# Two-layer hybrid token-mixing backbone: a weight split moved behind two stage borders, sixteen transposes moved ahead of another

## The reference

```python
for layer in range(DEPTH):
    p_lat = _split(_modulate(h_x, mod_lat[0], mod_lat[1]) @ w_in[layer], GROUP_COLS)
    p_ctx = _split(_modulate(h_c, mod_ctx[0], mod_ctx[1]) @ w_in[layer], GROUP_COLS)
    y_a = _rwkv7_mixer(p_ctx[0], p_lat[0], ...)
    y_b = _diff_attention(p_ctx[1], p_lat[1], ...)
    y_c = _hgrn2_mixer(p_ctx[2], p_lat[2], ...)
    y_d = _mlstm_mixer(p_ctx[3], p_lat[3], ...)
    # concatenated, @ w_out, residual norm, convolutional gated MLP, residual norm
```

## Time and profile before

| | |
|---|---|
| median of 3 runs | 1746.48 us (1746.31 to 1747.27) |
| the profiled execution | 1743.03 us |
| its span, first to last instruction | 1740.9 us |
| PE busy | 1595.0 us, 92% |
| DVE busy | 1089.4 us, 63% |
| ACT busy | 636.7 us, 37% |
| mean granted clock of TensorE | 0.956 of full speed |

### The profile page before, as it was taken

How to read it: one execution, slowest core, us unless ns; L and a number is a source line. 1 busy time by engine, 2 the same in 40 slices (tenths; PEclk the granted TensorE clock), 3 DMA queues, 4 the chain that set the end, 5 groups by cost and what they waited for, 6 DMA issues and landing times. The chain is left out here.

```text
span 1740.9 us, 29515 instructions
## 1 busy us (share of the span) xinstructions
PE 1595.0 (92%) x12140; PEld 1267.4 (73%) x12140; DVE 1089.4 (63%) x1870; ACT 636.7 (37%) x1060; POOL 75.5 (4%) x112
## 2 busy tenths in 40 slices
PE   6999999878889999999999979999977799899997
PEld 4766776655678778888888867677764587678885
DVE  2287347887786674554453364745678867578776
ACT  4255222333531245222222252433243431366662
POOL 0000011200101000000000000000020100000000
PEclk8999999978999999999999989999978899999998
DMA  9411111077301034222223022112225101255551
GB/s 391 149 49 50 49 61 52 22 250 247 136 3 51 26 146 154 104 96 92 102 84 119 1 87 86 61 49 85 74 86 178 68 3 51 77 212 197 186 203 47
DMA packets 41622, 182.02 MB, mean 105 GB/s; under 512 B 4753, under 2 KB 5521, under 8 KB 33681
## 3 DMA queue, kind: packets, MB, share of 16 engines
q1 hardware_dynamic: 41488, 180.14, 29.0%
HBM read 179.08 MB, written 1.05 MB: 103 GB/s over the span
## 5 line engine op out<-in xcount | busy, mean ns | idle before, releaser
L235 PE MATMUL ps<-hr_in,wr_in 128*128 128x512 f32 (+1 forms) x544 | 221.8, 408 | 14.4 <-DVE wr_in L228 13.9
L236 PE MATMUL ps<-hr_in,wr_in 128*128 128x512 f32 (+1 forms) x544 | 209.1, 384 | 0.0
L237 PE MATMUL ps<-hr_in,wr_in 128*128 128x512 f32 (+1 forms) x544 | 208.5, 383 | 0.0
L235 PEld LDWEIGHTS ps<-hr_in,wr_in 128*128 128x128 f32 x544 | 108.4, 199 | 63.9 <-issue 35.4
L228 DVE TENSOR_TENSOR wr_in<-mix,wr_in 128x1024 fp32r<-128x1024 f32 x68 | 83.8, 1234 | 93.5 <-ACT wr_in L224 89.6
L235 PE MATMUL ps<-mix_r,work_r 128*128 128x512 f32 (+1 forms) x352 | 133.8, 380 | 1.6 <-DVE work_r L228 1.6
L236 PE MATMUL ps<-work_r 128*128 128x512 f32 (+1 forms) x356 | 135.1, 379 | 0.0
L228 DVE TENSOR_TENSOR work_r<-pr,work_r 128x2048 fp32r<-128x2048 f32 x38 | 86.9, 2288 | 67.7 <-ACT work_r L224 63.6
L237 PE MATMUL ps<-mix_r,work_r 128*128 128x512 f32 x320 | 124.5, 389 | 0.0
L237 PEld LDWEIGHTS ps<-hr_in,wr_in 128*128 128x128 f32 x544 | 108.3, 199 | 19.6
L236 PEld LDWEIGHTS ps<-hr_in,wr_in 128*128 128x128 f32 x544 | 108.8, 200 | 15.5 <-issue 0.2
(11 more groups left out here) (525 smaller groups left out, 3312.1 us busy)
## 6 DMA issues: line engine op xcount, KB each, us to landing
mix<-in_w_in SPq DMA_DIRECT2D x68, 512.0 KB, 3.7
pr<-in_w_up SPq DMA_DIRECT2D x28, 1024.0 KB, 4.9
pr<-in_ada_w SPq DMA_DIRECT2D x40, 512.0 KB, 6.3
ring<-in_w_up SPq DMA_DIRECT2D x16, 1024.0 KB, 4.8
ring<-in_ada_w SPq DMA_DIRECT2D x28, 512.0 KB, 4.5
pr<-in_w_down SPq DMA_DIRECT2D x14, 1024.0 KB, 5.0
pr<-in_ada_w SPq DMA_DIRECT2D x8, 1024.0 KB, 15.6
work<-in_w_out SPq DMA_DIRECT2D x16, 512.0 KB, 4.1
```

What stands on the lines that cost most here:

```text
L235: nc.tensor.matmul(out, sh, mh, start=first, stop=False)
L236: nc.tensor.matmul(out, sh, ml, start=False, stop=False)
L237: return nc.tensor.matmul(out, sl, mh, start=False, stop=last)
```

## The change

Two edits. First, `high` and `low` of tile `end+1` leave the end of `front`, `diff_attention` and `mlstm`; `act_turn` and `dve_turn` now split tile `t+1` for a stage's first tile too, so the same instructions stand in turn 0 of the next stage. Second, the 8 transposes of `T_V` and the 8 of `ks` leave the head of `rwkv` and stand at the end of `hgrn`'s PE program, behind two waits (`kk_max`, `lora_out`). They write the same PSUM banks, 0 to 3. ACT's waits for them in `rwkv` go, since the border orders them.

```diff
@@ Projection @@
         for t in self.started(i):
             if t > self.first:
                 self.leave_act(act, t - 1)
-                self.high(act, t + 1)
+            self.high(act, t + 1)
...
             if t > self.first:
                 self.leave_dve(dve, t - 1)
-                self.low(dve, t + 1)
+            self.low(dve, t + 1)
@@ front @@
             for t in range(proj.end):
-                proj.low(dve, t + 2)
+                if t + 2 <= proj.end:
+                    proj.low(dve, t + 2)
...
             for t in range(proj.end):
-                proj.high(act, t + 2)
+                if t + 2 <= proj.end:
+                    proj.high(act, t + 2)
@@ diff_attention, and the same in mlstm @@
             proj.leave_dve(dve, proj.end - 1)
-            proj.low(dve, proj.end + 1)
...
             proj.leave_act(act, proj.end - 1)
-            proj.high(act, proj.end + 1)
@@ hgrn, end of PE @@
             late_job((2, 3))
+            pe.wait_ge(S("kk_max"), 1)
+            pe.wait_ge(S("lora_out"), 8)
+            for src, bank in ((tiles(pr, T_V, 2), 0), (R.ks, 2)):
+                for j in range(TILES):
+                    for i in range(2):
+                        nc.tensor.transpose(ps[bank + j // 2][:, (j % 2) * 256 + i * P:(j % 2) * 256 + (i + 1) * P],
+                                            src[:, i * T + j * P:i * T + (j + 1) * P], ident)
@@ rwkv, PE @@
-            turns(tiles(pr, T_V, 2), (0, 1)).then_inc(S("vT"), 1)
             turns(be, (6, 7)).then_inc(S("beT"), 1)
-            turns(ks, (2, 3)).then_inc(S("kT"), 1)
@@ rwkv, ACT @@
-            act.wait_ge(S("vT"), 1)
...
-            act.wait_ge(S("kT"), 1)
```

## The result

The changed kernel takes 1737.99 us (median of 4 runs, 1734.94 to 1740.96) where the kernel before takes 1746.88 (1746.31 to 1750.11). The ratio is 0.9945, with a 95% interval of 0.9924 to 0.9967. Timed twice more, it had ratios of 0.9961 [0.9943, 0.9978] and 0.9959 [0.9943, 0.9974] (brackets are 95% intervals throughout). By the medians it is faster by 7 to 9 us, where 11.2 were forecast. That is inside the range 1731.5 to 1740.5, but not inside the 1732 to 1737.5 that was given 0.59: 1738.0 lies in the band of the rival *half of it*.

What follows compares the result with a forecast made beforehand. PE, busy 92% of the span, was taken as the bound. Border gains of 4.75, 2.7 and 5.35 us made 12.8, less 1.6 for one low-clock stretch: 11.2 off 1746.48 gives 1735.3 us, range 1731.5 to 1740.5.

Steps and rivals of the forecast that it cites:

- half of it: Rival for the whole kernel: the clock falls as before after every border, gain 4.4 us, time 1742; chance 0.23.
- The border into `diff_attention`: Cast and subtraction leave the tail: restarts 1.35 and 1.7 us sooner, scores another 0.5 and 1.2; 4.75 us together.
- the second part: Behind the `diff_attention` border: the clock stays up after shorter idle, so scores come another 0.5 and 1.2 us sooner.
- the clock gain of layer 1: Behind layer 1's `diff_attention` border: full-rate clock brings the scores 1.2 us sooner; ends nothing and 1.5.
- The border into `mlstm`: PE restarts 2.2 us sooner per layer, but waits for a later `lf` at L1091; 2.7 us net of 4.4.
- After `lf` comes a serial chain and it shifts as a whole: In `mlstm` behind `lf`: gates, copies, scans and next split shift together, so the net 1.3 and 1.4 us stay.
- the cost at `lf` in full: Rival *no change*: 2.3 us cost at `lf` against 2.2 gained, `rwkv`'s head waits for something else; 1743.5 us, chance 0.05.
- The border into `rwkv`: Sixteen fewer transposes at PE's head let DVE's copy L2456 start sooner: 2.7 and 2.65 us, 5.35 together.
- sign of being wrong: Behind the `rwkv` border: the forecast is wrong if L2456 starts less than 1.8 us earlier.
- The cover of 1.95 us: End of layer 1's `hgrn`: PE ends 1.95 us before DVE, hiding the sixteen transposes at full clock; 0.05 us lost.
- The 1.6 us taken off for one low stretch: Deduction for one costly low-clock stretch, likeliest at PE's new wait for `lf` or the `rwkv` border; 1.6 us.

Runs made afterwards that it cites:

- filler run: The kernel before with two float32 filler matmuls on PE at the end of `front`, result not read; 1744.8 us, ratio 1.0011.
- transposes alone: The kernel before with only the second edit, the sixteen transposes moved to the end of `hgrn`; 1742.82 us, ratio 0.9974.
- second border alone: The changed kernel with the border into `diff_attention` as before, so only the border into `mlstm` and the transposes changed; 1744.05 us, ratio 0.9990.
- first border only: The changed kernel with the border into `mlstm` as before, so only the border into `diff_attention` and the transposes changed; 1736.3 us, ratio 0.9960.
- reordered kernel: The changed kernel with DVE making `lf` ahead of the moved subtraction in `mlstm`; 1727.55 us, ratio 0.9902, and again 1724.94 us, ratio 0.9876.
- Filling the wait: The changed kernel with two filler matmuls on PE ahead of its wait for `lf`; 1736.04 us, ratio 0.9947.

## Why the prediction was right, and where it was not

**The border into `diff_attention`: right in mechanism and nearly in size.** Said: restarts 1.35 and 1.7 us sooner, scores another 0.5 and 1.2; measured 1.57 and 1.32, then 0.73 and 1.45, 5.1 in all for 4.75. These restarts are mixed with the clock in `front`: PE's own idle stretches shrank by 1.48 and 1.78. The filler run shows that the second part is the clock. In layer 1 the distance alone says too much: two other profiles with the old tail (transposes alone, second border alone) had no fall behind the same 2.71 us of idle, and their scores came after 5.73 and 5.74 us too. Yet the transposes-only kernel needed 71.17 us from this restart to the next one, the kernel before 71.34: the clock had fallen elsewhere in the stage. With both borders changed, eight profiles of nine took 67.7 us. Of the 3.5 us less, 2.2 are owed to the later border, so 1.3 stay with the clock gain of layer 1. The moved subtraction put off the first maxima a little (from 1076.61 it ran 1.23 us, and they started at 1077.75) and nobody waited.

**The border into `mlstm`: the step that failed.** I said 2.7 us net, because PE came to L1091 1.3 and 1.4 us after `lf` was there, so only 0.9 and 0.8 of the late `lf` would count. In one profile against the other that is what stands there (0.85 and 0.71). But a stretch that starts sooner did not end sooner. "After `lf` comes a serial chain and it shifts as a whole" is the sentence that failed, and with it the 1.3 and 1.4 us.

The traces settle it if one counts to the broadcasts at the chain's end, from the moment when PE runs dry ahead of the border. In layer 1 the old order took 35.42, 35.71, 37.09 and 35.44 us (kernel before, transposes alone, first border only, filler), the changed order 35.52 to 35.57 in all seven of its profiles. In layer 0 the old order took 40.72, 37.88, 40.71 and 40.66 us, the changed order 39.36 to 42.50, with a mean of 41.2, in the six with the wait unfilled. So of the 2.2 us won at the border nothing is left at the broadcasts, save against one of four profiles in layer 1. Two things ate it:

- The wait for `lf`. Three of the four old profiles had the clock fall behind this border, and there PE had the 1.3 us to spare that I read. In the fourth it stayed up and the old order reached L1091 after 7.25 and 6.40 us. Against that one the new order's 9.32 and 8.47 are 2.07 us later, which by itself cancels the gain.
- The clock behind L1091. In layer 0 the wait of 2.4 us was followed by slower small matmuls in five profiles of six (3.22 to 4.01 us instead of 2.35). In layer 1 the stretch behind L1091 always had the longer low spell, 26.34 to 26.38 us against 24.74. Two old profiles had that too, so it is not bound to the new order.

The two runs with one border each point the same way, but only within the error: leaving this border alone costs nothing (0.9960 against 0.9959 and 0.9961), and changing it beside the transposes gives 0.9990 where the transposes alone gave 0.9974. I had named the rival, the cost at `lf` in full, and given it together with a failing `rwkv` only 5%.

That L1215 waits behind the subtraction is now shown. Its input, the logarithm, ended at 171.60; it started at 173.71, as soon as the subtraction let it. With the two exchanged it started at 170.52 right behind the logarithm. By the Trainium skill's rule ("TensorE: Matmul & The Clock Gate", section "Architectural detail: the array is 16× 32×32, not 1× 128×128": the queues of ScalarE and VectorE are strictly first in, first out) that is what must happen, and the trace agrees.

**The border into `rwkv`: right, sized a little high.** Said 2.7 and 2.65 us, or 1.8 at the lower clock; measured 1.74 (lower clock) and 2.61. The 1.74 is just under the 1.8 that the prediction had set as a sign of being wrong; the mechanism held, DVE's wait for the transposes fell to 2.42 and 1.56 us. Part of the size is the clock again. The old head took 5.39 us in five of its six cases, and 3.72 in the one at full clock; against that one the new head's 2.78 is 0.94 us sooner. Of the nine profiles with the transposes moved and no more matmuls put there, eight had the lower clock in layer 0 (3.61 to 3.69 us behind the border) and one had not (2.81). None had it in layer 1. The cover of 1.95 us ahead of layer 1's border was read rightly. In seven of the nine profiles the sixteen transposes use it up, and PE ends within 0.13 us of DVE; in the other two the cover was 3.3 us, where PE's last work ahead of the transposes (L446) ran at full clock.

**The 1.6 us taken off for one low stretch** stood in for all of this. It was too small, but it covered part of the 2.7 us that did not come. That the time landed in the range is in part luck: two borders came nearly as forecast, the third gave nothing, and the range was wide enough for that.

**What is left open.** The reordered kernel is 10 to 14 us faster than the changed one by the medians. 4.1 us are L1091's earlier start. From L1091 to the broadcasts the profiles give another 2 or so in layer 0 (27.45 to 29.09 against 29.10 to 32.2) and 1.6 in layer 1 (24.76 against 26.36). The rest of layer 0's `mlstm`, from the broadcasts to PE's restart in `hgrn`, took 142.2 to 142.3 us in all three profiles with `lf` first, 142.3 to 145.5 with the changed order, and 142.2 to 145.2 with the old one.

The mean granted clock of each execution says where the surplus lies, though not why. An estimate of what the lower level costs is the span times what the clock lacks to 1.00; it takes PE to be the bound throughout. Over the 28 executions of the changed kernel it is 77 us (mean clock 0.956, mean span 1735.9), over the twelve of the reordered one 68 (0.9605, 1724.7), over 90 of the kernel before 77 (0.956, 1743.6). So 9 of the 11 us between the changed and the reordered kernel are fewer or shorter spells at the lower level, while the change itself saved its 8 us in waiting and nothing by the clock that this estimate can see. Filling the wait won the clock right behind it in layer 0 only. Why `lf` first keeps the clock up in the rest of the kernel was not tested.

**A better version.** `lf` first: 0.9902 and 0.9876 of before. It is the change with two lines moved, the wait for the logarithm and the subtraction that makes `lf`.

## What to carry to other kernels

Work moved behind a border is not free because its own result is wanted late: look at what stands behind it in the same queue, and how late that may be. Slack read from one trace on a clocked-down engine may be gone in the next execution; ask what it would be at the full clock before paying with it. Count a gain to the end of the serial chain behind it, not to the chain's first link: here 2.2 us at the border were 1.4 at L1091 and nothing at the broadcasts. When a shortened wait and a new wait show up in one profile, put the moved work behind the instruction that ends the new wait.

## What the runs showed of the hardware

After idle stretches of 2.71 to 3.15 us the same code ran on at the lower clock in one execution and at the full clock in another: in the kernel before L1091 came 8.48 us behind the border, in the transposes-only kernel, with the same 3.15 us idle, 7.25. At `diff_attention`'s border the clock fell after 2.01 us of idle in three profiles of three, and after 2.71 in one of three. After 0.53, 0.93 and 0.99 us at these borders it stayed up in each profile. The places where the clock falls differ between executions of one kernel and move single stretches by 1.5 to 3 us, which fits the spread of 7 to 10 us over 12 executions of one kernel here. The restart behind the three borders took 0.30 to 0.33 us after the last engine in every case read.
